# Two output tiles of the out-projection begun on the retention and Fourier channels before the last attention block is transposed

## What is computed

```python
def reference(x, c, ctx, c_ctx, w_mod, ...):
    h = ctx
    for l in range(DEPTH):
        need_ctx = l < DEPTH - 1
        ...
        a_lat = modulate(x, norm1_g[l], mod_lat[0], mod_lat[1])
        a_ctx = modulate(h, norm1_g[l], mod_ctx[0], mod_ctx[1])
        m_lat, m_ctx = token_mixers(a_lat, a_ctx, w_in[l], w_out[l], ...)
        x = x + mod_lat[2] * m_lat
        x = x + mod_lat[5] * sq_relu_mlp(modulate(x, norm2_g[l], mod_lat[3], mod_lat[4]), w_ff1[l], w_ff2[l])
        if need_ctx:
            h = h + mod_ctx[2] * m_ctx
            h = h + mod_ctx[5] * sq_relu_mlp(modulate(h, norm2_g[l], mod_ctx[3], mod_ctx[4]), w_ff1[l], w_ff2[l])
    return x

def token_mixers(...):
    ...
    m_lat = jnp.concatenate([att_lat, ret_lat, four_lat], axis=-1) @ w_out
```

## Time and profile before

| | |
|---|---|
| median of three runs | 1770.08 us (1768.99 to 1774.89) |
| profiled execution, own time | 1762.71 us |
| its span | 1760.9 us |
| mean granted TensorE clock | 0.961 of full |
| TensorE busy with matmuls | 1637.2 us, 93% |
| TensorE busy with weight loads | 1411.1 us, 80% |
| VectorE busy | 1034.9 us, 59% |
| ScalarE busy | 573.6 us, 33% |
| GpSimd busy | 563.4 us, 32% |
| HBM read | 152.61 MB, 88 GB/s over the span |

### The profile page before, as it was taken

One profiled execution on the slowest core, in us unless ns is written; L12 is line 12 of the kernel. 1 busy time (PEld: TensorE's weight loads), 2 busy tenths in 40 slices (PEclk: granted clock), 3 DMA queues, 4 the chain that ended last, 5 costly groups with the idle time before them and its releaser, 6 DMA issues.

```text
span 1760.9 us, 23096 instructions
## 1 busy us (share of the span) xinstructions
PE 1637.2 (93%) x8912; PEld 1411.1 (80%) x8912; DVE 1034.9 (59%) x1462; ACT 573.6 (33%) x912; POOL 563.4 (32%) x312
## 2 busy tenths in 40 slices
PE   6799988989987999999999997997999799999998
PEld 6688877988876888888888886886898688888887
DVE  3758966784766766656656346286553554444442
ACT  1532244661242121221221226233563432222221
POOL 0234654001222222222232223335202344444442
PEclk9799999988998999999999997998899899999999
DMA  7233311102323434444443221221001233333332
GB/s 275 72 120 120 95 55 49 37 13 84 120 81 97 128 96 143 121 120 120 135 124 88 71 60 48 72 78 55 1 1 49 58 98 96 96 95 91 92 93 94
DMA packets 159400, 155.95 MB, mean 89 GB/s; under 512 B 6336, under 2 KB 123728, under 8 KB 159312
## 3 DMA queue, kind: packets, MB, share of 16 engines
q1 hardware_dynamic: 159312, 154.72, 28.7%
HBM read 152.61 MB, written 2.10 MB: 88 GB/s over the span
## 4 chain that ended last, share of the span: by engine, by line
PE 81%; DVE 10%; ACT 4%; issue 3%; DMA 1%; SPq 1%; POOL 0%; DVEq 0%; ACTq 0%; POOLq 0%
PE psA L1618 26%; PE psB L1618 26%; PE ps L1587 3%; PE psS L1286 2%; PE ps L1286 2%; PE psA L1405 2%; PE psA L1406 1%; PE psA L1407 1%; PE psB L1405 1%; PE psB L1407 1%; PE psB L1406 1%; PE psS L1346 1%; DVE Ab L1219 1%; DVE scr L1005 1%; DVE macc L827 1%
## 5 line engine op out<-in xcount | busy, mean ns | idle before, releaser
L448 POOL TENSOR_TENSOR Wlo<-raw,Whi 128x1024 fp32r<-128x1024 f32 x172 | 418.4, 2433 | 1052.4 <-ACT Whi L559 1052.4
L559 ACT ACTIVATE Whi<-raw 128x1024 fp32r<-128x1024 f32 x180 | 190.7, 1060 | 743.1 <-PE psB L1618 333.7
L1219 DVE TENSOR_TENSOR Ab<-Tb 128x768 f32<-128x768 f32 (+1 forms) x64 | 158.7, 2480 | 186.5 <-ACT Tb L768 186.5
L1618 PE MATMUL psA<-Ahi,Whi 128*128 128x512 f32 x480 | 148.9, 365 | 14.5 <-DVE Alo L878 6.1
L1618 PE MATMUL psA<-Alo,Whi 128*128 128x512 f32 x480 | 146.7, 360 | 0.0
L1618 PE MATMUL psA<-Ahi,Wlo 128*128 128x512 f32 x480 | 146.3, 359 | 0.0
L1618 PE MATMUL psB<-Ahi,Whi 128*128 128x512 f32 x480 | 144.7, 356 | 0.0
L1618 PE MATMUL psB<-Alo,Whi 128*128 128x512 f32 x480 | 144.6, 355 | 0.0
L1618 PE MATMUL psB<-Ahi,Wlo 128*128 128x512 f32 x480 | 144.3, 355 | 0.0
L1618 PE MATMUL psA<-Hhi,Whi 128*128 128x512 f32 (+1 forms) x384 | 116.6, 358 | 8.7 <-DVE X L983 8.7
L827 DVE SCALAR_TENSOR_TENSOR macc<-modraw,csil,macc 128x512 f32<-128x512 f32 x112 | 108.9, 1030 | 18.1 <-DMA modraw<-in_w_mod_dram 18.0
(11 more groups left out here) (300 smaller groups left out, 3339.9 us busy)
## 6 DMA issues: line engine op xcount, KB each, us to landing
raw<-in_w_ff_dram SPq DMA_DIRECT2D x128, 512.0 KB, 4.1
modraw<-in_w_mod_dram SPq DMA_DIRECT2D x72, 512.0 KB, 4.2
raw<-in_w_in_dram SPq DMA_DIRECT2D x36, 512.0 KB, 3.7
modst<-in_w_mod_dram SPq DMA_DIRECT2D x16, 512.0 KB, 5.1
raw<-in_w_out_dram SPq DMA_DIRECT2D x16, 512.0 KB, 4.3
modat<-in_w_mod_dram SPq DMA_DIRECT2D x8, 512.0 KB, 3.8
modraw<-in_dft_lat_dram SPq DMA_DIRECT2D x8, 257.0 KB, 3.7
Xin<-in_x_dram SPq DMA_DIRECT2D x4, 512.0 KB, 10.2
```

What stands on the lines that cost most here:

```text
L448: nc.gpsimd.tensor_tensor(Wlo[:, s, :], raw[:, s, :], Whi[:, s, :], ALU.subtract).then_inc(S["lo_done"], 1)
L559: nc.scalar.activation(Whi[:, slot, :], raw[:, slot, :], ACT.Copy).then_inc(S["hi_done"], 1)
L1219: V.tensor_tensor(Ab[:, k % 2, 0:w], Tb[:, k % 2, 0:w], Tb[:, k % 2, 0:w], ALU.mult).then_inc(S["h_full"], 1)
L1618: last = mm(dst[:, c0:c0 + cn], wt, x[:, i, c0:c0 + cn], start=f, stop=e)
```

## The change

TensorE's program alone is changed, in both layers. The attention loop stops before the last block's scaling and transposes. TensorE then multiplies channel blocks 4 to 7 of tile 0 into `psA`, transposes `AO`, multiplies channel blocks 4 to 7 of tile 1 into `psB`, waits for `aoT_lo`, and finishes the two tiles with blocks 0 to 3 in the loop over u. The sum over the channel blocks is thus made in another order for these two tiles. The other six tiles are as before, and so are the programs of the other engines.

```diff
             keep_clock(ps7, WARM)
-            for s in range(2, n_items + 5):
-                attention(s)
-            pe.wait_ge(S["aoT_lo"], l * NT + TT[l])
-
             def tile(dst, slot, offs, hi_, lo_, opens=True, closes=True):
...
             k8 = [k * P for k in range(KT)]
+
+            def mixed(u, ks):
+
+                return tile(pair[u % 2], (u0 + UP + u) % 2, k8[ks], Ahi[:, ks], Alo[:, ks], ks.start == 4, ks.start == 0)
+
+            for s in range(2, n_items + 3):
+                attention(s)
+            pe.wait_ge(S["rT_lo"], l * NT + TT[l])
+            pe.wait_ge(S["y_lo"], 2 * l + (2 if l == 0 else 1))
+            for u in range(2):
+                pe.wait_ge(S["lo_done"], u0 + UP + u + 1)
+                if u:
+                    attention(n_items + 3)
+                    attention(n_items + 4)
+                mixed(u, slice(4, 8))
+            pe.wait_ge(S["aoT_lo"], l * NT + TT[l])
+
             for u in range(UO):
                 uu = u0 + UP + u
                 pe.wait_ge(S["lo_done"], uu + 1)
-                if u >= 2:
+                if u < 2:
+                    mixed(u, slice(0, 4)).then_inc(S["lin_ready"], 1)
+                else:
                     pe.wait_ge(S["resid_done"], 72 * l + u - 1)
-                tile(pair[u % 2], uu % 2, k8, Ahi, Alo).then_inc(S["lin_ready"], 1)
+                    tile(pair[u % 2], uu % 2, k8, Ahi, Alo).then_inc(S["lin_ready"], 1)
```

## The result

| | before | after |
|---|---|---|
| median of 15 runs | 1769.33 us (1759.63 to 1785.12) | 1758.97 us (1753.43 to 1768.29) |
| ratio of the runs | | 0.9946, 95% interval 0.9919 to 0.9972 |
| profiled execution | 1762.71 us | 1768.29 us |
| its span, mean granted clock | 1760.9 us, 0.961 | 1766.5 us, 0.957 |

The change makes the kernel faster by 10.4 us at the median, and by 5 to 14 us within the interval. Three slow executions among the later runs (4749.37 us of before, 2087.30 us of e2_layer0, 1782.25 us of e9_after) are left out of all means and ratios. The profiled execution of after is the slowest of its 15, so the two spans can't be compared. The places of the change can.

What follows compares the result with a forecast made beforehand. TensorE was taken to set the pace, with 81% of the chain. Gains of 3.0 us in layer 1 and 2.8 us in layer 0 sum to 5.8 us, so 1770.08 - 5.8 = 1764.3 us; range 1760 to 1769.5 us.

Steps and rivals of the forecast that it cites:

- Layer 1, the waits and the clock: At layer 1's attention end, half tiles cover both TensorE waits (2.25 us gained) and keep the clock full (1.73 us).
- Layer 1, a new wait: At tile 2 of layer 1, TensorE waits 0.97 us for weights that only half of tile 1 now covers.
- The stop that the forecast leaned on: A 1.50 us stop amid dense tiles, stretch from 602.50, left the clock at 1.00; so no clock cost was added.
- Layer 0, the waits: At layer 0's attention end, the waits of 0.86 and 1.41 us around the transposes go: 2.27 us gained.
- Layer 0, the clock: After layer 0's last values, the low clock stays 5.08 us at unchanged price; only faster transposes gain 0.45 us.
- rival 3: The clock gives more, in layer 0's low level or layer 1's saved stretch: gain 7 to 9 us; chance 0.14.
- Layer 0, what comes late next: Tile 0 ends 1.28 us later; VectorE's second modulation piece, clear of GpSimd's low part, shrinks from 4.89 to 3.0 us.
- 1: The clock gives less, in layer 0 or layer 1: gain only 2 to 4 us; chance 0.20.
- 2: VectorE's stretched 4.89 us operations stay, tile 3 of layer 0 waits 0.9 us: gain 4.9 us; chance 0.10.
- 4: The first half tile finds an operand not ready and waits as long as before: 1770.1 us; chance 0.03.
- 5: Layer 0's modulation load lands late and becomes the bound, TensorE waits at tile 3: 1771.1 us, slower; chance 0.03.
- The range: Whole kernel: 1760 us (gain of 9 less a microsecond of scatter) to 1769.5 us (gain of 2 plus as much).

Runs made afterwards that it cites:

- e2_layer0: The change applied in layer 0 alone, against the kernel before; ratio of the whole 0.9960 (0.9924 to 0.9996).
- e9_after: The changed kernel measured a third time, against the kernel before; ratio of the whole 0.9978 (0.9951 to 1.0005).
- e4_dummy: The kernel before plus idle matmuls, results overwritten, in its two waits (4 before, 6 behind the transposes); ratio to the kernel before 0.9979 (0.9947 to 1.0012).
- e3_layer1: The change applied in layer 1 alone, against the kernel before; ratio of the whole 0.9978 (0.9945 to 1.0010).
- e8_before: The kernel before, unchanged, for a second profile; one run, layer 0's stretch 36.66 us and layer 1's 21.50 us.
- e1_again: The changed kernel once more, for a second profile, against the kernel before; ratio of the whole 0.9947 (0.9924 to 0.9969).
- e6_first: The changed kernel without tile 1's early half, so nothing stands behind the transposes; ratio to the kernel before 0.9962 (0.9925 to 1.0000).

## Why the prediction was wrong

- **Layer 1, the waits and the clock** (2.25 and 1.73 us): right. The stretch is 3.2 us shorter, forecast 3.0. The price of the clock by itself was 1.5 us (e4_dummy). The 1.73 us also held some 0.3 us that are not the clock's: a tile behind a wait takes 5.73 us at full clock too (tile 2 in after), and 5.74 in e4_dummy. That 0.3 us now stands at tile 2, and is largely made good by the transposes, which cost 0.44 us between two half tiles (414.90 to 415.34 in layer 0) where 0.66 stood between the waits.
- **Layer 1, a new wait** (0.97 us): right, 0.95 us in each of the four profiles to within 0.01, with no fall of the clock. The stop that the forecast leaned on for this was 1.34 us, not 1.50: its stretch holds 0.16 us of work.
- **Layer 0, the waits** (2.27 us): right; e4_dummy leaves 2.2 us for them.
- **Layer 0, the clock** (0.45 us): this step failed. It read "So the low stretch stays, it only begins to be used at 398.66", from one profile in which the clock had fallen 1.7 us ahead of the values' end. The runs show that the low stretch under tile 0 belonged to the waits. Where layer 0 stands as before, the clock is low for tile 0 also when it was full at the values (e3_layer1, e8_before), and filling the waits alone gives it back (2.9 us, e4_dummy). With the waits gone, it stays full in three profiles of four and costs 0.8 us in the fourth, where it fell 1.8 us ahead of the values' end, as in the profile that the forecast was read from. What the forecast listed as a bound, 2.71 us gained, was near what happened, and rival 3, at 0.14, is what came. The layer is worth 5.1 us, not 2.8.
- **Layer 0, what comes late next**: right in its mechanism. The second modulation piece took 2.74 us in all four profiles with layer 0 changed and 4.89 to 4.95 in the three with it as before. The Trainium skill's rule (page SBUF — State Buffer, "Who interferes with whom"), that the two engines block each other as a whole, fits: in after the VectorE operations begin at 433.16, when GpSimd's had ended at 432.50. But tile 0 did not end 1.28 us later: from the last scores it ended at +17.1 instead of +18.8, for the clock was full.
- **The rivals**: 1, 2, 4 and 5 did not come. No load landed late, and no operand was missing.
- **The range**: with the clock of layer 0 the sum would have been 8.3 us and the forecast 1761.8. The median measured first, 1758.97, is 2.8 us below even that. The later measurements of the same kernel, 10.8 and 4.3 us by the means, show such a distance to be scatter; one microsecond for it at the range's end was too little, for kernels whose runs have a standard deviation of 4 to 7 us. So the 10.4 us of the first measurement are in part luck of the draw; the two places account for 8.3.

## What to carry to other kernels

A wait of TensorE can cost twice: its length, and slow matmuls behind it. Two waits of 0.85 and 1.4 us, with one set of transposes between them, came with a low clock for the next tile at all six places where they stood; a single one of 0.95 or 1.4 us amid dense tiles left it full, also at six places. Where the clock is already low ahead of a wait, that is no proof that it would be low without it: compare several executions, or fill the wait with matmuls that nobody reads, which prices the clock alone. And when a tile is split so that its first part covers a wait, look at what the second part was covering; here it was the weights of the tile after next, and two blocks ahead instead of four were the better cut, by 0.65 us in layer 1.

## What the runs showed of the hardware that was not expected

- At a granted clock of 1.00 the same tile of 48 matmuls takes 8.32 us in some executions and 8.48 in others. Both occur within one execution too, in groups of four tiles: before has 8.32 us for the four from 751.50 on and 8.48 for the four from 818.94 on. The rows are tile 3 of layer 0, of e1_again and of after, which is the same kernel:

```profile
428.85 8.32 PE psB L1614 x48
```

```profile
438.23 8.48 PE psB L1614 x48
```

In after more of the tiles take 8.48 us than in before, and layer 0's feed-forward part is 4.8 us longer (541.14 to 1060.29 before, 549.56 to 1073.49 after: 519.2 and 523.9 us). What chooses between the two is open.
- How long the clock stays low under dense matmuls is not fixed: 5.1, 5.9 and 6.1 us of tile 0 in the three unchanged profiles of layer 0, 2.9 to 3.4 us in the three of layer 1 (3.1 in before, where the earlier trace rows show the first 2.92), 1.6 us in e2_layer0 and e6_first. The Trainium skill (page TensorE: Matmul & The Clock Gate, "What's actually happening") says that the monitor runs freely, and the spread agrees. A fixed price per fall would be wrong.
- A low clock can last: in the profile of after TensorE was busy all the 22 us from 268 to 290, at 0.50, where before it was at 1.00 with 20.1 us busy. It got through 108 matmuls there against 178. In e9_after it was so too, from 265.7 to 289.6, and its last scores of layer 0 came at 406.28. That being busy the whole time did not bring the clock back is what surprised; what would have is not tested. After's last scores came 12.5 us later than before's, more than the whole change gives.
- The fall ahead of that stretch stands at a wait of 2.75 us that all twelve profiles have. In before, where the clock stayed at 1.00, and in after, where it fell:

```profile
265.29 0.72 PE L1503 MATMUL psA<-rqT,rkT 64*128 64x128 f32 x8 [2.75 <-DVE Alo L1103]
```

```profile
266.45 1.23 PE L1503 MATMUL psA<-rqT,rkT 64*128 64x128 f32 x8 [2.75 <-DVE Alo L1103]
```

The clock fell in the four profiles in which this wait ended latest (266.39 to 266.75) and stayed in the eight in which it ended at 264.93 to 266.32. So the same wait does not always drop it. The four are those with the change whole in layer 0 (after, e1_again, e2_layer0, e9_after), but nothing in the program ahead of the wait differs; whether the change has a part in this is not shown.
